# Each expert finishes its own slots: residual rows gathered, normed rows scattered to the output, no combining stage

## The chip, the cores and the metric

One Trainium2 chip, one of its cores. The metric is the device time of one launch in microseconds (us), the median of the runs. The core has a matmul engine (PE, TensorE), a vector engine (DVE), an activation engine (ACT), a general engine (POOL) and a queue that mostly issues transfers (SP). Transfers run on 16 DMA engines that all queues share.

## The reference, cut to what matters

One layer (attention, pooling branch, gated merge) over 576 tokens (512 of a prompt, 64 of samples), width 1024, then a mixture of 32 experts of width 512, two experts for each token. All float32. What the change touches is this end of it:

```python
h  = x + m @ w_out                               # merged branches, residual
xt = rms_norm(h, ffn_norm_g)
g_sel = argmax(xt @ w_router_group + b)          # 4 groups; softmax weight g_w
top_v, top_i = top_k(logits of that group, 2)    # two experts of its 8
e_w = softmax(top_v) * g_w
...
hb = silu(xt[tok] @ w_exp_gate[e]) * (xt[tok] @ w_exp_up[e])
yb = (hb @ w_exp_down[e]) * e_w                  # for each token and chosen expert
h  = h + sum of the token's two yb
y  = rms_norm(h, final_norm_g)                   # y_prompt, y_sample
```

The 32 experts have 1152 assignments, 36 on the mean. The weights of one expert are three blocks (gate, up, down) of 2,048 KB, 192 MiB for all.

## The kernel before, in words

Everything is written by hand for each engine, with semaphores; the order on an engine is the order in the code. The part before the experts (projections, attention, gates, output product) isn't touched, except for a few loads.

**Routing.** For five tiles of 128 tokens, `add_residual` writes h into `resid`; `route` forms the logits. Of the same h, ACT (`xs2`) and POOL (`xn2`, L1821) form the normed rows and POOL stores them to a DRAM tensor `xn2_d` (L1825). DVE chooses experts (`first_of`), ranks each token within its expert, and PE turns that into a table by slot (L991, semaphore `tok_done`): 64 slots (`CAP`) for each expert, and for each slot the row of `xn2_d`. `rowx` and `rowy` are these tables. A slot without a token holds an index out of bounds, for which the transfer moves no row. A branch for experts with over 64 tokens (`over > CAP`) exists and isn't taken on this data.

**Experts.** Expert c uses buffer set s = c mod 2 (`M[s]` holds its semaphores). Rows are handled as halves: partition p < 64 is the first half (512 numbers) of slot p, partition 64 + p the second. For each expert the engines do, in this order:

- POOL `gather_x` (L1701): an indirect DMA of the 128 half rows into `xg[s]`. It is issued as soon as PE has turned the rows of expert c - 2 that were in `xg[s]` (`xt_done`).
- PE `turn_x` (L1001, four transposes), ACT copies to `xT` (L1309).
- PE `gate_up` (L1018): both products into one bank. ACT `silu` (L1313), DVE product (L1647), PE `turn_h` (L1026), ACT copy (L1317), PE `down` (L1033).
- DVE copies the result to `yo[s]` (L1651, semaphore `y_ev`), POOL `scatter_y` (L1705) stores it to its slots in a DRAM tensor `y_d`.

On PE, `turn_x` of expert c + 1 stands between `gate_up` and `turn_h` of expert c. The weights of expert c + 2 are loaded by SP: gate and up (L498, L500) when `gate_up` of expert c is done, down (L503) when `down` of expert c is done. At the start, expert 2's gate goes to a place of its own (`wg2`), its up to `wu2`.

**Combining.** After expert 31, POOL gathers for each of the five tiles the token's two rows of `y_d` (`combine`, L1698, ten indirect DMAs), DVE adds them with their weights to `resid` (L1669), ACT forms the sum of squares and its root (L1350, L1352), DVE the normed rows (L1676), SP stores them (L555).

## Time and profile before

| | |
|---|---|
| median of 3 runs | 1116.12 us (1114.67 to 1117.65) |
| the profiled execution | 1115.16 us, its span 1113.5 us |
| busy in the span: PE, DVE, ACT, POOL | 944.4, 338.7, 201.7, 198.3 us |
| granted TensorE clock, mean | 0.951 of full speed |
| first gate and up product starts | 597.0 us |
| last down product ends | 1079.9 us |
| combining stage, to the end of the span | 33.6 us |

The page of the profile gives busy times over the whole span; which limit holds in which stage is read from the windows, the waits and the timeline.

### The profile page before, as it was taken

To read this page: it belongs to the slowest core of one execution; us is meant where nothing else is said; L and a number is where in the kernel's file an instruction comes from. 1 tells how busy PE (TensorE), PEld (TensorE's weight loads), DVE (VectorE), ACT (ScalarE), POOL (GpSimd) and SP (SyncE) were. 2 spreads that over 40 slices of the span, in tenths; PEclk is the share of its full clock that TensorE was granted. 3 is DMA by queue.
4 is the path that set the end of the run, shared out by engine and by line. 5 is a ranking of instruction groups with operands and counts; after the bars stand their busy time and mean duration, and the time that the engine had idled before them with its cause. 6 is when DMAs were issued, how large, how long until landed. Compare 5 with 4: busy or idle time off the path is not lost.

```text
span 1113.5 us, 11556 instructions
## 1 busy us (share of the span) xinstructions
PE 944.4 (85%) x4412; PEld 510.2 (46%) x4412; DVE 338.7 (30%) x743; ACT 201.7 (18%) x445; POOL 198.3 (18%) x296
## 2 busy tenths in 40 slices
PE   7978999999999998999976998788778887887770
PEld 6633444767776566774543433333233333333220
DVE  2269999973331111330143100000000000000006
ACT  3243111213344233000121000000000000000012
POOL 2730650100001200000231121111110111011113
PEclk9989999999999999999996999999999999899995
DMA  9920221610204527913035999999999999999937
GB/s 335 392 78 1 76 85 38 231 39 38 76 1 152 203 100 216 378 64 150 38 126 227 408 419 426 421 424 425 426 423 424 424 425 425 421 425 425 422 136 252
DMA packets 51814, 283.72 MB, mean 255 GB/s; under 512 B 8476, under 2 KB 9344, under 8 KB 32823
## 3 DMA queue, kind: packets, MB, share of 16 engines
q1 hardware_dynamic: 40935, 246.21, 55.0%
q0 software_dynamic: 10784, 36.97, 9.2%
q8 instruction: 25, 0.41, 0.2%
q14 instruction: 14, 0.11, 0.0%
q10 hardware_dynamic: 56, 0.01, 0.0%
HBM read 267.38 MB, written 23.17 MB: 261 GB/s over the span
## 4 chain that ended last, share of the span: by engine, by line
PE 64%; DVE 18%; issue 7%; ACT 4%; DMA 3%; SPq 2%; POOL 1%; ACTq 0%; POOLq 0%; DVEq 0%
PE psum L1018 21%; PE psum L1033 11%; PE psum L780 9%; DVE arena L1421 6%; DVE arena L1419 6%; PE psum L934 5%; PE psum L916 3%; PE psum L604 3%; DMA arena<-in_w_branch_pool 2%; PE psum L1026 1%; PE psum L868 1%; DVE arena L1647 1%; ACT arena L1313 1%; ACT arena L1317 1%; PE psum L834 1%
## 5 line engine op out<-in xcount | busy, mean ns | idle before, releaser
L1018 PE MATMUL psum<-arena 128*64 128x512 f32 x992 | 238.9, 637 | 56.5 <-issue 55.6
L1018 PEld LDWEIGHTS psum<-arena 128*64 128x64 f32 x992 | 86.2, 147 | 207.5 <-issue 207.5
L1033 PE MATMUL psum<-arena 128*64 128x512 f32 x512 | 116.9, 597 | 17.7 <-ACT arena L1317 17.7
L780 PE MATMUL psum<-arena 128*128 128x288 f32 x480 | 126.1, 416 | 0.0
L780 PEld LDWEIGHTS psum<-arena 128*128 128x128 f32 x480 | 89.6, 192 | 31.0 <-issue 8.1
L1647 DVE TENSOR_TENSOR arena<-arena,psum 128x256 f32<-128x256 f32 x32 | 13.5, 421 | 292.1 <-ACT arena L1313 292.1
L1313 ACT ACTIVATE arena<-psum 128x256 f32<-128x256 f32 x32 | 12.3, 384 | 418.1 <-PE psum L1018 407.3
L590 PE MATMUL psum<-arena 128*128 128x512 f32 x192 | 86.2, 604 | 2.1 <-ACT arena L1184 2.1
L1033 PEld LDWEIGHTS psum<-arena 128*64 128x64 f32 x512 | 40.4, 136 | 72.1 <-issue 72.1
L1651 DVE COPY arena<-psum 128x512 f32<-128x512 f32 x32 | 22.1, 691 | 157.1 <-PE psum L1033 157.1
L916 PE MATMUL psum<-arena 128*128 128x288 f32 x256 | 64.3, 415 | 3.7 <-DMA arena<-in_w_branch_pool 3.7
L1419 DVE MAX8 arena<-arena 64x8 f32<-64x1032 f32 (+3 forms) x80 | 66.2, 828 | 2.8
L1845 POOL CAST arena<-arena 128x1 int32 x30 | 5.6, 185 | 329.7 <-DVE arena L1651 329.7
L1421 DVE MATCH_REPLACE8 arena<-arena 64x1032 f32<-64x1032 f32 (+3 forms) x76 | 61.9, 814 | 0.0
L916 PEld LDWEIGHTS psum<-arena 128*128 128x128 f32 x256 | 49.5, 194 | 18.5 <-DMA arena<-in_w_branch_pool 4.6
L590 PEld LDWEIGHTS psum<-arena 128*128 128x128 f32 x192 | 36.3, 193 | 45.1 <-issue 42.8
L934 PE MATMUL psum<-arena 128*128 128x512 f32 x128 | 55.8, 593 | 1.1 <-issue 1.1
L1091 ACT COPY arena<-psum 128x512 f32<-128x512 f32 (+6 forms) x106 | 47.0, 490 | 53.8 <-PE psum L807 31.8
L1701 POOL DMA_INDIRECT arena<-xn_d,arena x32 | 33.4, 1043 | 33.8 <-POOL arena L1839 25.9
L1705 POOL DMA_INDIRECT y_d<-arena x32 | 33.2, 1037 | 29.0 <-POOL arena L1845 27.4
L934 PEld LDWEIGHTS psum<-arena 128*128 128x128 f32 x128 | 23.9, 190 | 29.7 <-issue 29.7
L1821 POOL TENSOR_TENSOR arena<-arena 128x1024 f32<-128x1024 f32 (+1 forms) x5 | 11.7, 2344 | 139.0 <-ACT arena L1301 139.0
(263 smaller groups left out, 930.8 us busy)
## 6 DMA issues: line engine op xcount, KB each, us to landing
arena<-in_w_exp_down SPq DMA_DIRECT2D x32, 2048.0 KB, 22.9
arena<-in_w_exp_gate SPq DMA_DIRECT2D x31, 2048.0 KB, 18.2
arena<-in_w_exp_up SPq DMA_DIRECT2D x30, 2048.0 KB, 22.6
arena<-in_w_in SPq DMA_DIRECT2D x7, 2048.0 KB, 8.6
y_d<-arena SPq DMA_DIRECT2D x1, 8192.0 KB
arena<-in_x_prompt SPq DMA_DIRECT2D x8, 512.0 KB, 7.2
arena<-in_w_out SPq DMA_DIRECT2D x2, 2048.0 KB, 10.4
arena<-in_w_exp_up SPq DMA_DIRECT2D x4, 1024.0 KB, 12.8
```

The costliest lines, as they stand in the source:

```text
L590: last = pe.matmul(bank(b, n, slice(0, r)), lhs, w[:, k, 0:n], start=(k == 0), stop=(k == KD - 1))
L604: last = pe.matmul(out, lhs, wqi[:, k, QIH * half:QIH * half + QIH], start=(k == 0), stop=(k == KD - 1))
L780: last = pe.matmul(bank(2 + n % 2 if n < SAMPLE_G else 2, HN), ring[slot % 2][:, k, m * P:(m + 1) * P], xnT[:, k, HN * hh:HN * hh + HN], s ...
L916: last = pe.matmul(bank(b, HN), w[:, 4 * br + k, m * P:(m + 1) * P], src[:, k, tc], start=(k == 0), stop=(k == 3))
L934: last = pe.matmul(bank(4 + 2 * (i % 2) + half), sgA[k][:, i * P:(i + 1) * P], ring[(R_OUT + half) % 2][:, k, :], start=(k == 0), stop=(k ...
L1018: last = pe.matmul(bank(2 + s, 512, rows).rearrange("p (w n) -> p w n", w=2), x_k, wgu[s][:, :, DE * k + 256 * q:DE * k + 256 * q + 256], ...
L1033: last = pe.matmul(bank(4 + s, 512, slice(64 * half, 64 * half + 64)), hT[s][:, k % 2, CAP * (k // 2):CAP * (k // 2) + CAP], wd[s][:, k, 5 ...
L1091: last = act.copy(out, src(b))
L1419: link(dve.max(m8, src))
L1421: link(dve.match_replace(w, m8, src, LOW))
L1701: pool.indirect_dma_start(xg[s], None, xn2_d, bass.IndirectOffsetOnAxis(ap=sidx[s], axis=0), bounds_check=2 * NT - 1, oob_is_err=False).th ...
L1705: pool.indirect_dma_start(y_halves, bass.IndirectOffsetOnAxis(ap=syid[s], axis=0), yo[s], None, bounds_check=2 * FIRST - 1, oob_is_err=Fal ...
```

## The change

The sum of the two experts and the final norm move into the expert loop. A token's expert with the lower number ("first visit") adds its weighted result to h and stores the sum to `y_d` at the slot that the token has in its second expert; the expert with the higher number ("second visit") gathers that row as its base, adds its own result, norms it and scatters it straight to the output.

- `xn2_d` is gone: h itself is stored (`h_d`). POOL's five products and ACT's five scalings go; norm factor and expert weight of each slot reach the experts as a table (`weights`, `cur[s]`), made by a second pass of small products on PE (`by_slot`, semaphores `qv_ready`, `qv_done`); silu and the product with up take the norm factor as a scale. The gain is applied as `xT` is written, now by DVE (`take_x`).
- `turn_x`: 16 products of 64x64 in place of 4 transposes of 128x128.
- In the loop, new: `gather_b` (base rows into the same `xg[s]`, after `xt_done`; a first visit's base rows are the h rows that `gather_x` brought), the addition on DVE (L1702 of the new kernel; waits for `b_in`), Square on ACT, `pair_sum` on PE (adds the two half rows' sums; it stands in the middle of the next expert's `gate_up`), Sqrt on ACT, reciprocal and product on DVE, two scatters `scatter_out` (prompt rows, sample rows). Gone: `combine` and all behind it.
- `gather_x` of expert c + 2 now waits for `y_ev` of expert c, since `xg[s]` is read by the addition. `gather_b` of expert c + 1 waits for the landing of `scatter_y` of expert c (`y_st`).
- SP: the rest of expert 1's and expert 2's up weights are loaded without waiting for the row store or the first gathers; expert 2's down (`wd2`) and expert 3's gate (`wg3`) get places of their own and are loaded once `xg_in` of expert 1 has come.

```diff
-            load_expert(1, 0, gate=False, up=False)
...
+            sp.dma_start(by_half(wd2), d_v[2]).then_inc(M[0]["wd_in"], 16)
+            sp.wait_ge(M[1]["wg_in"], 16)
+            sp.dma_start(flat(wg3), g_v[3]).then_inc(M[1]["wg_in"], 16)
...
+                    if prev is not None and k == 4:
+                        pair_sum(*prev)
...
+            def norm(m, s, n, c):
+                act.wait_ge(m["y_ev"], n + 1)
+                act.activation(bank(7), yo[s], ACT.Square, accum_out=sse[:, s:s + 1]).then_inc(S["sq3"], 1)
+                act.wait_ge(S["ps3"], c + 1)
+                act.activation(rte[:, s:s + 1], bank(6, 1, at0=s), ACT.Sqrt, bias=eps, scale=1.0 / D).then_inc(S["rt3"], 1)
...
+            def expert_y(m, s, n, c):
                 dve.wait_ge(m["y_done"], n + 1)
+                dve.wait_ge(m["b_in"], 16 * (n + 1))
...
+                dve.scalar_tensor_tensor(yo[s], bank(4 + s), cur[s][:, 0:1], xg[s], ALU.mult, ALU.add).then_inc(m["y_ev"], 1)
+                dve.wait_ge(S["rt3"], c + 1)
+                dve.reciprocal(rse[:, s:s + 1], rte[:, s:s + 1]).then_inc(S["rs3"], 1)
...
+                dve.scalar_tensor_tensor(fo[s], yo[s], rse[:, s:s + 1], fg2, ALU.mult, ALU.mult).then_inc(m["fin"], 1)
...
+                if more == 2:
+                    pool.wait_ge(M[s]["xt_done"], n + 1)
+                    pool.sem_inc(S["passed"], 1)
+                    pool.tensor_copy(sidx[s], rowx[:, bass.ds(c + 2, 1)]).then_inc(S["sidx_set"], 1)
+                    pool.wait_ge(S["sidx_set"], 2 * c + 2)
+                    pool.wait_ge(M[s]["y_ev"], n + 1)
                     pool.sem_inc(S["passed"], 1)
                     gather_x(s, M[s]["xg_in"])
...
+                scatter_y(s, M[s]["y_st"], FIRST)
+                if more == 2:
+                    pool.tensor_copy(cur[s], weights[:, bass.ds(c + 2, 1), :].squeeze(1)).then_inc(M[s]["c_set"], 1)
+                if more:
+                    if s or not first:
+                        pool.wait_ge(M[t]["o_st"], 32 * (n + s))
+                        pool.sem_inc(S["passed"], 1)
+                    pool.tensor_copy(so[t], rows4[:, bass.ds(c + 1, 1), :].squeeze(1)).then_inc(S["sidx_set"], 1)
+                    pool.wait_ge(S["sidx_set"], 2 * c + 3 if more == 2 else 2 * c + 2)
+                    pool.wait_ge(M[t]["xt_done"], n + s + 1)
+                    pool.wait_ge(M[s]["y_st"], 16 * (n + 1))
                     pool.sem_inc(S["passed"], 1)
+                    gather_b(t, M[t]["b_in"], FIRST)
+                pool.wait_ge(M[s]["fin"], n + 1)
+                pool.sem_inc(S["passed"], 1)
+                scatter_out(s, M[s]["o_st"])
```

POOL in the loop over pairs of experts, first half of the body, before (L1701 is `gather_x` of expert c + 2, L1705 `scatter_y` of expert c; xt_done0 and y_ev0 are those of expert c):

```order
L1839 ISA [waits xt_done0]
L1839 COPY arena<-arena 128x1
L1840 ISA
L1701 DMA arena<-xn_d,arena 128x512 [waits sidx_set]
L1845 ISA [waits y_ev0]
L1845 COPY arena<-arena 128x1
L1846 REGISTER_ALU
L1705 DMA y_d<-arena 36864x512 [waits sidx_set]
```

The same place now (L1756 `gather_x` of expert c + 2, L1764 `scatter_y` of expert c, L1760 `gather_b` of expert c + 1, L1769 the two `scatter_out` of expert c):

```order
L1906 ISA [waits xt_done0]
L1756 DMA arena<-h_d,arena 128x512 [waits sidx_set,y_ev0]
L1764 DMA y_d<-arena 36864x512
L1916 COPY arena<-arena 128x2
L1921 ISA [waits o_st1]
L1921 COPY arena<-arena 128x4
L1924 REGISTER_ALU [waits xt_done1,sidx_set]
L1760 DMA arena<-y_d,arena 128x512 [waits y_st0]
L1769 DMA out<-arena 1024x512 [waits fin0]
L1769 DMA out<-arena 128x512
```

The gather moved from before the wait for `y_ev` to behind it, and a gather stands behind a wait for the scatter's landing; an expert has five indirect DMAs in place of two.

DVE in the loop now, one expert (L1694 product with up, L1670 `take_x` of the next expert, L1702 the addition, L1709 the normed row); before, these were L1647 and L1651 alone:

```order
L1694 SCALAR_TENSOR_TENSOR arena<-psum,arena 128x256 [waits silu0]
L1670 TENSOR_TENSOR arena<-psum,arena 128x512 [waits xt_done1]
L1698 REGISTER_ALU [waits y_done0]
L1700 REGISTER_ALU [waits b_in0]
L1702 SCALAR_TENSOR_TENSOR arena<-psum,arena 128x512 [waits y_st0]
L1704 RECIPROCAL arena<-arena 128x1 [waits rt3]
L1709 SCALAR_TENSOR_TENSOR arena<-arena 128x512 [waits o_st0]
```

The result of an expert now waits for its base rows (`b_in`), which before no engine did.

## Rows read from the trace of the kernel before

**Rows 1.** Windows: 20 experts in mid-loop, then the combining stage; columns in the first row.

```profile
core 0: us, PE busy (x) PEld busy (x) DVE busy (x) ACT busy (x) POOL busy (x), PEclk, DMA share, GB/s
718.84:1034.44 315.60, 251.36 (x1080) 98.14 (x1080) 22.25 (x40) 26.86 (x60) 49.28 (x80) 0.95 1.01 424
...
1080.00:1113.50 33.50, 0.00 (x0) 0.00 (x0) 20.05 (x21) 7.22 (x15) 12.33 (x12) 0.55 0.66 216
```

**Rows 2.** Waits of PE from 700 to 1080 us: total, times, longest.

```profile
PE psum L1018 <- issue: 53.0, 22, 3.3
```

**Rows 3.** Timeline of one expert, mid-loop: start, us, engine, line, idle before.

```profile
1036.61 1.04 POOL L1705 DMA_INDIRECT y_d<-arena  x1 [0.91 <-POOL arena L1845]
1037.51 7.09 PE L1018 MATMUL psum<-arena 128*64 128x512 f32 x32 [3.07 <-issue]
...
1038.71 1.04 POOL L1701 DMA_INDIRECT arena<-xn_d,arena  x1 [0.86 <-POOL arena L1839]
1044.53 0.75 PE L1001 MATMUL psum<-arena 128*128 128x128 f32 x4
...
1045.62 0.48 PE L1026 MATMUL psum<-arena 128*128 128x128 f32 x2 [0.34 <-DVE arena L1647]
...
1046.65 3.65 PE L1033 MATMUL psum<-arena 128*64 128x512 f32 x16 [0.55 <-ACT arena L1317]
...
1050.34 0.69 DVE L1651 COPY arena<-psum 128x512 f32<-128x512 f32 x1 [4.87 <-PE psum L1033]
```

**Rows 4.** Timeline of SP: weight loads issued in the first 100 us of experts.

```profile
595.97 0.33 SPq L518 DMA_DIRECT2D arena<-in_w_exp_up  x1
596.34 0.43 SPq L519 DMA_DIRECT2D arena<-in_w_exp_up  x1
606.71 0.33 SPq L523 DMA_DIRECT2D arena<-in_w_exp_gate  x1
```

**Rows 5.** Line L1701 (`gather_x`), all 32: time from issue to landing.

```profile
DMA to landing us min/median/max: 2.9/8.9/9.8
```

**Rows 6.** Line L1705 (`scatter_y`), all 32: time from issue to landing.

```profile
DMA to landing us min/median/max: 2.4/8.1/8.8
```

**Rows 7.** Line L1701, window 597 to 598: the gather issued at 597.5.

```profile
DMA to landing us min/median/max: 6.2/6.2/6.2
```

**Rows 8.** Line L1705, window 1069 to 1070: the scatter of expert 30.

```profile
DMA to landing us min/median/max: 4.5/4.5/4.5
```

**Rows 9.** Timeline from the slot table to the end of the first gate and up product.

```profile
588.07 2.35 PE L991 MATMUL psum<-arena 128*64 128x32 f32 x40 [2.15 <-DVE arena L1607]
...
591.16 0.32 DVE L1612 TENSOR_TENSOR arena<-arena 128x160 f32<-128x160 f32 x1
...
594.47 0.17 DVE L1638 TENSOR_SCALAR arena<-arena 128x5 f32<-128x5 f32 x1
594.68 0.16 DVE L1640 TENSOR_TENSOR arena<-arena 128x5 f32<-128x5 f32 x1
...
595.16 1.10 PE L1001 MATMUL psum<-arena 128*128 128x128 f32 x4 [4.74 <-DMA arena<-xn_d,arena]
...
597.03 9.65 PE L1018 MATMUL psum<-arena 128*64 128x512 f32 x32 [0.77 <-ACT arena L1309]
```

**Rows 10.** Timeline of the end: last down product, combining stage.

```profile
1076.26 3.65 PE L1033 MATMUL psum<-arena 128*64 128x512 f32 x16 [0.55 <-ACT arena L1317]
1076.67 1.28 ACT L1343 ACT_TABLE_LOAD   x1 [0.56 <-issue]
...
1079.95 0.69 DVE L1651 COPY arena<-psum 128x512 f32<-128x512 f32 x1 [4.86 <-PE psum L1033]
...
1084.64 0.97 POOL L1698 DMA_INDIRECT arena<-y_d,arena  x1 [0.30 <-issue]
...
1097.77 1.03 ACT L1350 ACTIVATE psum<-arena 128x1024 f32<-128x1024 f32 x1 [19.60 <-DVE arena L1669]
...
1098.95 0.29 ACT L1352 ACTIVATE arena<-arena 128x1 f32<-128x1 f32 x1
```

More of the change, by code:

```diff
@@ L304, in program @@
         o = SG + 128
[L305 to L306 removed]
+        trash = at(W1 - D, D)
         xn2T = [at(o + 3 * D + s * D, KD, P) for s in range(2)]
@@ L999, in turn_x, with pair_sum, gate_up @@
                 pe.sem_inc(S["passed"], 1)
-                for t in range(KD // 2):
-                    last = pe.transpose(bank(0, P, at0=t * P), xg[s][:, t:KD // 2 * (P - 1) + t + 1:KD // 2], ident)
+                for k in range(KD):
+                    for half in range(2):
+                        rows = slice(CAP * half, CAP * half + CAP)
+                        last = pe.matmul(bank(0, CAP, rows, k * CAP), xg[s][rows, k:KD * (CAP - 1) + k + 1:KD], ident[rows, rows], start=True, stop=True)
                 last.then_inc(m["xt_done"], 1)
-            def gate_up(m, s, n, third=False, halves=False):
+            def pair_sum(s, c):
+                pe.wait_ge(S["sq3"], c + 1)
+                pe.matmul(bank(6, 1, at0=s), pairs, sse[:, s:s + 1], start=True, stop=True).then_inc(S["ps3"], 1)
+            def gate_up(m, s, n, gate=None, up=None, halves=False, prev=None):
                 pe.wait_ge(m["xt_ev"], n + 1)
@@ L1638, in _ @@
[L1638 to L1644 removed]
+            dve.tensor_tensor(top2, const("valid"), top1, ALU.subtract)
+            dve.tensor_tensor(w1, w1, const("valid"), ALU.mult)
@@ L1651, in expert @@
-                dve.tensor_copy(yo[s], bank(4 + s)).then_inc(m["y_ev"], 1)
-            for s in range(2):
-                expert(M[s], s, 0)
-            with dve.Fori(1, NE // 2) as i:
-                for s in range(2):
-                    expert(M[s], s, i, 16 * i)
+                dve.wait_ge(m["b_in"], 16 * (n + 1))
+                if not (isinstance(n, int) and n == 0):
+                    dve.wait_ge(m["y_st"], 16 * n)
+                dve.sem_inc(S["passed"], 1)
+                dve.scalar_tensor_tensor(yo[s], bank(4 + s), cur[s][:, 0:1], xg[s], ALU.mult, ALU.add).then_inc(m["y_ev"], 1)
@@ new lines, in _, with expert @@
+            pool.wait_ge(M[0]["xt_done"], 1)
+            gather_b(0, M[0]["b_in"], FIRST)
+            def expert(s, n, more=2):
+                c = 2 * n + s
+                t = 1 - s
+                first = isinstance(n, int) and n == 0
+                if more == 2:
[4 more added lines that the diff above has]
+                    pool.wait_ge(M[s]["y_ev"], n + 1)
@@ L1853, in _ @@
-                scatter_y(s, M[s]["y_st"])
-            pool.wait_ge(S["dest_ready"], 1)
+                expert(s, 0)
+            with pool.Fori(1, NE // 2 - 1) as i:
+                for s in range(2):
+                    expert(s, i)
+            expert(0, NE // 2 - 1, 1)
+            expert(1, NE // 2 - 1, 0)
+            for s in range(2):
+                pool.wait_ge(M[s]["y_st"], 16 * (NE // 2))
+                pool.wait_ge(M[s]["o_st"], 32 * (NE // 2))
             pool.wait_ge(S["flag_ready"], 1)
```

499 lines of the change are left out of this document (264 added, 235 removed).

## The prediction

> **What bounds the kernel now.** The windows come first. In mid-loop 20 experts take 315.6 us, 15.78 each, with a DMA share of 1.01 at 424 GB/s [rows 1]. An expert's three weight blocks are 6.29 MB, at 424 GB/s 14.84 us; so 0.94 us of each 15.78 goes to one gather and one scatter. PE isn't the bound: in each expert it waits about 3 us ahead of `gate_up` (53.0 us in 22 times, [rows 2]), put down to "issue", because the weights' landing isn't seen as a releaser. Its own work is 7.09 + 0.75 + 0.48 + 3.65 with gaps, from 1037.51 to 1050.30 in the timeline, 12.8 us [rows 3]. POOL's transfers are off the path: a scatter takes 8.1 us at the median to land and a gather 8.9 [rows 5, 6], but nobody waits for the scatter, and the gather issued at 1038.71 lands some 9 us later for a `turn_x` that is due with the next expert. Behind the last down product (ends 1079.9) stands the combining stage, 33.6 us to the end of the span, nothing else beside it [rows 1, 10].
>
> **The end: removed and added.** The stage is gone. In its place, after expert 31's down product: addition 0.1 + 0.7 (as L1651), Square of half the width of L1350's 1.03, so 0.6 with 0.2 for its sum; then a table load of 1.28 (the Sqrt isn't in silu's table; `pair_sum` lies beside it), Sqrt 0.3, reciprocal 0.15, product 0.7; POOL's pick-up 0.9 (the 0.91 ahead of a DMA in [rows 3]); two scatters, the second 0.97 + 0.30 after the first [rows 10]; landing 2.4, the value without weight traffic [rows 6]; about 1 of gaps. That is 0.85 to the sum and some 9.5 from there. Alone this would save 33.6 - 10.4 = 23 us.
>
> **The start.** The slot table is out of PE at 590.4 and read by 590.9. Then DVE has about 19 small operations, half of them chained at 0.2 apart, and six products of 160 columns at 0.32 or, unchained, a little less: 2.8 + 1.6, `qv_ready` at 595.3 [rows 9]. PE's second pass is 40 products like L991's (2.35 us for 32 columns; now 96, I take 2.6): 598.1. It stands ahead of `turn_x`. Then 16 small products 1.1 (L991's pace, 59 ns each, would give 0.94) and `take_x` 0.7 + 0.2: the first `gate_up` at 600.1 in place of 597.03, +3.1. It takes the same 9.65 [rows 9]: done at 609.8. From `turn_x` to the end of `down` is 5.8 us [rows 3]; 16 products for 4 transposes add 0.4: 6.2. Addition 0.9. Expert 0's sum is ready ("y") at 616.9. POOL's five products and ACT's scalings were beside the routing on DVE and PE: nothing.
>
> **The loop: two circles that the change closes.** Before, no transfer of expert c waited for a result of expert c - 1. Now POOL does, from y of expert c: pick-up 0.9; issue of `gather_x`(c+2) 1.04; 0.3; issue of `scatter_y`(c) at 2.25; **its landing**; pick-up 0.9; `gather_b`(c+1), **its landing**; then 0.85 for the addition: y of c + 1. With unloaded landings (2.4, 2.9) that is 9.3 us. With loaded ones: the scatter now follows a gather by 1.35 us, and of two such transfers the second lands 2.9 us after the first (issued 2.10 apart in [rows 3], landing 8.1 and 8.9), so its own landing takes 9.5; the gather takes 8.1: 2.25 + 9.5 + 0.9 + 8.1 + 0.85 = 21.6 us. The second circle: y of c, 0.9, `gather_x`(c+2) lands (8.1 loaded), `turn_x` to `down` of c + 1 6.3, 0.85: 16.2 loaded, 11.0 unloaded. PE's own work grows to 13.2.
>
> The DMA engines need 14.84 + the small ones. Five in place of two, three of them half filled: between 0.94 + 0.17 (by bytes) and 5 x 0.47 (by number), I take 1.5: 16.3 us for an expert.
>
> Neither 21.6 nor 9.3 can last. At 21.6 the engines would be idle 5.3 us of each, and the landings short; below 16.3 the queue fills up and the landings grow. I lay out one round from y of c. The `pair_sum` wait holds `gate_up`(c+1) in its middle until y + 1.3, its second half is 3.55, so gate and up of c + 3 are issued at y + 4.9 and flow from about 6. If the queue has just run empty before, at 5.5 to 6, gather and scatter land with its end, near 6.8. How a landing shrinks as the backlog ends is seen twice: 6.2 for the gather issued 1.2 us behind two half blocks, 4.5 for the scatter of expert 30 behind the last down block [rows 4, 7, 8]. But `gather_b` is issued at 6.8 + 0.9, into 9.9 us of gate and up, and is fully loaded: 15.8. Then 0.85: y of c + 1 at 16.7. An idle half microsecond on top of 16.3 is what this needs, so the round settles at **16.8 us**. The bounds: 14.8 (landing at 4.8, as unloaded, the gather still loaded) and 21.6.
>
> ACT's table loads (1.28 each, [rows 10], now two an expert) lie in its idle time: silu's is done before `gate_up` ends, Sqrt's while PE is busy; if not covered, up to 1.3 us an expert. `scatter_out` is issued while `gather_b` is under way, so POOL isn't late; it only lengthens the queue. Behind POOL's wait for the landing stand `gather_b` and both `scatter_out`; DVE waits for the former, and through `pair_sum` so does PE.
>
> **Preloads.** Two blocks are 9.9 us of DMA work, moved into the stretch 596 to 607, which holds only the two half blocks now [rows 4]. Where the DMA bounds the loop they are a gain of that size. Where the circle does, they leave the queue empty during experts 1 to 4, which then run at PE's 13.0: 4 x 3.8 = 15 us less.
>
> **Sum.** 616.9 + 31 x 16.8 - 15 + 9.5 = 1132 us of span; the execution's own time is 1.7 above its span (1115.16 to 1113.5), and lies 1.0 below the median: about **1134 us**, 1.6% slower. In terms of before: -23 at the end, +4 to expert 0's sum, +38 from there to expert 31's.
>
> **A rule against the trace.** The landings of the small transfers have medians of 8.1 and 8.9 us under weight traffic and minima of 2.4 and 2.9 [rows 5, 6]. The Trainium skill (DMA: Bandwidth & Descriptors, section Anatomy of one DMA) gives a transfer of this kind as about 2.0 us plus bytes over 436 GB/s, an estimate of 2.3 for the 147 KB of 36 rows. By it the first circle would be 2.25 + 2.3 + 0.9 + 2.3 + 0.85 = 8.6 and never bind; the medians here contradict that, the minima agree. The same page (Issuing engines are not separate DMA queues) has transfers of all queues interleave on the same 16 engines, as the medians suggest.
>
> **Rivals.**
> *The circle hides behind the DMA, faster.* If landings shrink enough (half-empty transfers, idle moments), the loop stays DMA-bound. The last down product ends at 1079.9 now [rows 10]; -9.9 by the preloads, +0.5 x 27 for added traffic, +3 from the later start: it ends about 1087, + 0.85 + 9.5 = 1097, time **1099**. For it: the DMA share of 1.01 says only the queue counts now. Against: it needs the circle under 16.3 with a queue that never empties, in which both landings take over 8. It decides where the two landings together are below 12.3 us. Chance 0.25.
> *The circle is fully loaded, slower.* If the queue's weight packets hold each small transfer its full 8 to 9 us even where the engines are partly idle, 19 to 21.6 a round: 616.9 + 31 x 20 - 20 + 9.5, time **1228**. Chance 0.09.
> *No change.* A circle of 16.2 gives 1115. Chance 0.06.
> My forecast has 0.60.
>
> **Range.** Rounds of 16.3 to 18.0 give 1118 to 1171; with the hidden circle's 1092 to 1105 below, the range is 1092 to 1178; the rest (0.2) is mostly the fully loaded case. The likeliest case's own range is 1120 to 1170. This kernel's measurement tells 0.3%, 3.3 us, from no change. Faster 0.27, same 0.06, slower 0.67.
>
> **What the new profile would show.** Right: in mid-loop a DMA share of 0.95 to 0.98 and rounds near 16.8; DVE's addition waiting for the landing of `gather_b`; PE waiting at `pair_sum`'s line, not ahead of `gate_up`; `scatter_y` landing in some 5 us, `gather_b` in 8; first `gate_up` at 600; 10 us from the last down product to the end. Wrong: a share of 1.00 with PE waiting ahead of `gate_up` (then the circle hides), or `scatter_y` still at 8 us and more beside idle engines (then 20 us rounds).

## The result and the profile after

The changed kernel takes 1187.39 us (median of 4 runs, 1185.81 to 1188.49), the kernel before beside it 1115.72 (1114.67 to 1117.65): ratio 1.0642, 95% interval 1.0628 to 1.0656. It is slower by 71.7 us where 18 were forecast. Its profiled execution has a span of 1186.7 us. One of the four executions of experiment 1 below took 2507 us; the time given there, 1155.8 us, is the median of the other three.

The same stretch of mid-loop as in [rows 1], by windows (PE, PEld, DVE, ACT and POOL busy, granted clock, DMA share, GB/s):

```profile
718.84:1034.44 315.60, 266.21 (x1460) 114.94 (x1460) 48.53 (x87) 75.09 (x120) 99.19 (x138) 0.88 0.93 367
```

The DMA engines, full before at 1.01 and 424 GB/s, now have gaps (0.93, 367), and TensorE's granted clock has fallen from 0.95 to 0.88. So something waits; the question is in which circle.

The addition that makes an expert's sum y (L1702), all 32, by the view of one line: its duration and first and last start, then what ended VectorE's idle time before it:

```profile
L1702 DVE SCALAR_TENSOR_TENSOR arena<-psum,arena x32: 750/751/752, 616.4 to 1171.5; 128x512 f32<-128x512 f32 x32
its engine sat idle before it (us, times) until:
  DMA arena<-y_d,arena: 116.9, 17
  PE psum L1061: 87.5, 15
```

These rows give the two facts on which the rest stands. From the first to the last y are 555.1 us, 31 rounds of **17.91 us**. And 17 times y waited last for `gather_b` (the first circle), 15 times for `down` on TensorE. By the timeline (expert 0's y ends no round) the 17 rounds that end with `gather_b` take 18.5 us at the mean (16.2 to 20.6), the 14 others 17.2 (13.3 to 19.0). Two successive rounds of mid-loop, timeline (start, us, engine, line, idle before):

```profile
871.86 0.75 DVE L1702 SCALAR_TENSOR_TENSOR arena<-psum,arena 128x512 f32<-128x512 f32 x1 [7.17 <-DMA arena<-y_d,arena]
...
873.42 0.38 PE L1027 MATMUL psum<-arena 128*128 128x1 f32 x2 [1.38 <-ACT psum L1349]
873.48 1.06 POOL L1756 DMA_INDIRECT arena<-h_d,arena  x1 [6.57 <-DVE arena L1702]
...
874.85 1.02 POOL L1764 DMA_INDIRECT y_d<-arena  x1 [0.31 <-issue]
...
880.14 2.18 PE L1022 MATMUL psum<-arena 64*64 64x64 f32 x32 [2.75 <-DMA arena<-h_d,arena]
881.03 1.06 POOL L1760 DMA_INDIRECT arena<-y_d,arena  x1 [4.74 <-DMA y_d<-arena]
...
883.70 6.61 PE L1061 MATMUL psum<-arena 128*64 128x512 f32 x16 [0.75 <-ACT arena L1345]
...
890.49 0.75 DVE L1702 SCALAR_TENSOR_TENSOR arena<-psum,arena 128x512 f32<-128x512 f32 x1 [6.66 <-PE psum L1061]
...
898.82 2.14 PE L1022 MATMUL psum<-arena 64*64 64x64 f32 x32 [1.17 <-DMA arena<-h_d,arena]
899.89 1.05 POOL L1760 DMA_INDIRECT arena<-y_d,arena  x1 [5.08 <-issue]
...
901.94 3.65 PE L1061 MATMUL psum<-arena 128*64 128x512 f32 x16 [0.55 <-ACT arena L1345]
...
908.46 0.75 DVE L1702 SCALAR_TENSOR_TENSOR arena<-psum,arena 128x512 f32<-128x512 f32 x1 [6.53 <-DMA arena<-y_d,arena]
```

The first round (18.63 us) runs over the second circle: `gather_x` issued 0.9 behind y, `turn_x` held up 2.75 by it, then `down` in 6.61 us, and y right behind. The second round (17.97) runs over the first circle: `gather_b` issued at 899.89, y 8.57 later, while `down` had taken 3.65 and was long done. The windows of four TensorE pieces (`turn_x` and `down` of the first round, part of `gate_up` and `down` of the second) show where the 3 us between the two `down` come from:

```profile
880.10:882.30 2.20, 2.16 (x33) 2.08 (x33) 0.00 (x0) 0.00 (x0) 1.06 (x1) 0.50 0.94 402
883.70:890.13 6.43, 6.43 (x16) 2.03 (x18) 0.14 (x1) 0.00 (x0) 1.18 (x2) 0.53 0.93 385
895.00:897.60 2.60, 2.60 (x14) 0.62 (x10) 0.48 (x1) 0.74 (x1) 0.00 (x0) 1.00 0.95 394
901.94:905.40 3.46, 3.46 (x17) 1.41 (x19) 0.00 (x0) 0.00 (x0) 1.49 (x3) 1.00 1.04 440
```

Behind the 2.75 us of waiting the granted clock is 0.50 to 0.53 (1.2 GHz); behind the 1.17 us it is 1.00 (2.4 GHz). `turn_x` takes 2.1 us at either.

TensorE's own waits over 24 experts (700 to 1150 us) are nearly all for `gather_x`, ahead of `turn_x`; those at `pair_sum` (L1027), for the y of the expert before, are few:

```profile
PE psum L1022 <- DMA arena<-h_d,arena: 45.1, 24, 3.4
PE psum L1027 <- ACT psum L1349: 6.8, 6, 3.1
```

The landings are shorter than those of [rows 5, 6]. By the view of line L1756 from 700 to 1060 us, `gather_x`:

```profile
DMA to landing us min/median/max: 4.0/6.5/7.4
```

And by that of L1764, `scatter_y`:

```profile
DMA to landing us min/median/max: 2.8/5.3/7.4
```

The end, by the timeline:

```profile
1175.00 0.75 DVE L1709 SCALAR_TENSOR_TENSOR arena<-arena 128x512 f32<-128x512 f32 x1 [0.17 <-DVE arena L1704]
1176.62 0.98 POOL L1769 DMA_INDIRECT out<-arena  x1 [2.48 <-DVE arena L1709]
1177.91 0.98 POOL L1769 DMA_INDIRECT out<-arena  x1 [0.30 <-issue]
```

And by the view of line L146, where each engine's program ends, POOL's row (duration in ns, start):

```profile
L146 POOLq DRAIN  x1: 4709/4709/4709, 1181.7 to 1181.7; - x1
```

From the last y (done at 1172.3) to the end of the span are 14.4 us, 4.7 of them POOL's closing drain.

### The profile page after: what moved, and what is told of

It is laid out like the page before. It is cut to its first block, busy times and chain, and to the rows that moved or that the text cites. A ratio compares the mean times of both kernels' runs of the same rounds, so it can differ in the third digit from the quotient of the medians.

```text
span 1186.7 us, 14414 instructions
## 1 busy us (share of the span) xinstructions
PE 1031.5 (87%) x5444; PEld 569.7 (48%) x5444; DVE 373.9 (32%) x830; ACT 284.0 (24%) x550; POOL 279.9 (24%) x407
## 4 chain that ended last, share of the span: by engine, by line
PE 40%; DMA 30%; DVE 17%; issue 6%; ACT 2%; SPq 2%; POOL 1%; POOLq 1%; DVEq 0%; ACTq 0%
DMA arena<-y_d,arena 12%; DMA y_d<-arena 9%; PE psum L793 8%; PE psum L1061 6%; DVE arena L1441 6%; DVE arena L1439 6%; DMA arena<-h_d,arena 5%; PE psum L947 5%; PE psum L929 3%; PE psum L1022 3%; PE psum L617 2%; DMA arena<-in_w_branch_pool 2%; DVE arena L1702 2%; PE psum L1045 2%; DMA arena<-in_w_in 1%
## 5 line engine op out<-in xcount | busy, mean ns | idle before, releaser
L1045 PE MATMUL psum<-arena 128*64 128x512 f32 x960 | 219.7, 599 | 0.9 <-DVE arena L1670 0.9
L1061 PE MATMUL psum<-arena 128*64 128x512 f32 x512 | 162.5, 792 | 26.8 <-ACT arena L1345 25.0
L1022 PE MATMUL psum<-arena 64*64 64x64 f32 x1024 | 68.8, 290 | 51.5 <-DMA arena<-h_d,arena 51.5
L793 PEld LDWEIGHTS psum<-arena 128*128 128x128 f32 x480 | 89.4, 192 | 30.9 <-issue 8.3
L1022 PEld LDWEIGHTS psum<-arena 64*64 64x64 f32 x1024 | 64.8, 212 | 77.1 <-issue 77.1
L1702 DVE SCALAR_TENSOR_TENSOR arena<-psum,arena 128x512 f32<-128x512 f32 x32 | 24.0, 751 | 204.4 <-DMA arena<-y_d,arena 116.9
L1756 POOL DMA_INDIRECT arena<-h_d,arena x32 | 34.0, 1062 | 217.8 <-DVE arena L1702 186.8
L1349 ACT ACTIVATE psum<-arena 128x512 f32<-128x512 f32 x32 | 19.2, 601 | 225.4 <-DVE arena L1702 225.4
L1769 POOL DMA_INDIRECT out<-arena x64 | 63.8, 997 | 21.7 <-issue 19.2
L1760 POOL DMA_INDIRECT arena<-y_d,arena x32 | 33.9, 1058 | 148.4 <-DMA y_d<-arena 137.8
L929 PEld LDWEIGHTS psum<-arena 128*128 128x128 f32 x256 | 49.5, 194 | 19.5 <-DMA arena<-in_w_branch_pool 5.7
L603 PEld LDWEIGHTS psum<-arena 128*128 128x128 f32 x192 | 35.7, 190 | 44.0 <-issue 41.7
L1670 DVE TENSOR_TENSOR arena<-psum,arena 128x512 f32<-128x512 f32 x32 | 22.1, 692 | 100.6 <-PE psum L1022 95.6
```

The lines of the kernel that those rows point to most:

```text
L603: last = pe.matmul(bank(b, n, slice(0, r)), lhs, w[:, k, 0:n], start=(k == 0), stop=(k == KD - 1))
L793: last = pe.matmul(bank(2 + n % 2 if n < SAMPLE_G else 2, HN), ring[slot % 2][:, k, m * P:(m + 1) * P], xnT[:, k, HN * hh:HN * hh + HN], s ...
L929: last = pe.matmul(bank(b, HN), w[:, 4 * br + k, m * P:(m + 1) * P], src[:, k, tc], start=(k == 0), stop=(k == 3))
L1022: last = pe.matmul(bank(0, CAP, rows, k * CAP), xg[s][rows, k:KD * (CAP - 1) + k + 1:KD], ident[rows, rows], start=True, stop=True)
L1045: last = pe.matmul(bank(2 + s, 512, rows).rearrange("p (w n) -> p w n", w=2), x_k, wgu[s][:, :, DE * k + 256 * q:DE * k + 256 * q + 256], ...
L1061: last = pe.matmul(bank(4 + s, 512, slice(64 * half, 64 * half + 64)), hT[s][:, k % 2, CAP * (k // 2):CAP * (k // 2) + CAP], w[:, k, 512 * ...
```

## The experiments

Theory A: the first circle (y, `scatter_y`, its landing, `gather_b`, its landing, y) sets the round. Theory B: the second (y, `gather_x`, its landing, `turn_x`, `down`, y). Theory C: TensorE's clock or the traffic of the small transfers. Ratios are to the kernel before, with 95% intervals; a round is the time from first to last y over 31, from the row of its line; "last wait" is how often y waited last for `gather_b` and for `down`, from the same view.

**1. Four gather buffers.** `gather_x` no longer needs y to free its buffer (POOL's loop is written out for it).

```
...
-                    pool.wait_ge(M[s]["y_ev"], n + 1)
-                    gather_x(s, M[s]["xg_in"])
+                    gather_x(s, M[s]["xg_in"], 1 - par)
...
+                pool.wait_ge(M[s]["y_ev"], n + 1)
                 scatter_y(s, M[s]["y_st"], FIRST)
```

> Changed kernel with four gather buffers for the residual rows instead of two, so gather_x of the expert after next is issued before the wait for y (POOL's expert loop is written out, the work is the same). Theory A (the circle y, scatter_y, its landing, gather_b, y sets the round of 17.9): scatter_y now stands directly behind the wait for y, 1.3 us earlier, and circle 2 is gone: rounds 16.6, 1187 - 31 x 1.3 = 1147 us. Theory B (circle 2: y, gather_x, turn_x, down, y sets the round, since turn_x waits 51 us in all for gather_x): that wait goes, rounds fall to the 15.8 of the kernel before, 1187 - 31 x 2.1 = 1122. Theory C (TensorE at the lower clock, or the traffic of five small transfers, sets the round): 1187 within 5.

1155.8 us, 1.0375 (1.0351 to 1.0399); round 16.93. Last wait `gather_b` 28 times, `down` 4: the first circle alone, as A has it. The time lies 9 us above what A gave and 34 above B. `scatter_y` is issued 1.4 us earlier behind y, but takes 1.0 longer to land (line of `scatter_y`, 700 to 1060 us):

```profile
DMA to landing us min/median/max: 5.2/6.3/7.1
```

So issuing it earlier is worth less than the 1.3 us that the expectation took off.

**2. `scatter_y` ahead of `gather_x`** (the two lines change places behind the wait for y).

> Changed kernel with one swap on POOL's queue: scatter_y is issued before gather_x and not behind it. Theory A (circle over scatter_y's landing): scatter_y 1.3 us earlier, 1187 - 31 x 1.3 = 1147 us. Theory B (circle over gather_x and turn_x): gather_x is 1.2 us later, so 1187 + 31 x 1.2 = 1224. Theory C (clock or traffic): 1187 within 5. Both circles near 17 us: between 1165 and 1190, and clearly above the kernel with four gather buffers.

1210.3 us, 1.0858 (1.0839 to 1.0876); round 18.59. The addition's last waits in this kernel, all 32:

```profile
  PE psum L1061: 170.8, 30
  DMA arena<-y_d,arena: 10.7, 2
```

This is slower than A alone (1147) or both circles near 17 us (1165 to 1190) allowed, and 14 us less than B alone gave (1224). The second circle, with `gather_x` 1.3 us later, took nearly every round: A alone is wrong, and the prediction's second circle is too short. The first hardly got shorter, for the landing of `scatter_y` grew from a median of 5.3 us (same view):

```profile
DMA to landing us min/median/max: 6.1/6.2/8.1
```

**3. No landing in the first circle.** `scatter_y` writes another tensor, and `gather_b` doesn't wait for it; left out is what a token's first expert passes on to its second.

```
...
+        z_d = nc.dram_tensor("z_d", (SLOTS, D), F32, kind="Internal").ap()
...
-                pool.indirect_dma_start(y_halves, ...
+                pool.indirect_dma_start(z_halves, ...
...
-                    pool.wait_ge(M[s]["y_st"], 16 * (n + 1))
                     gather_b(t, M[t]["b_in"], FIRST)
```

> Changed kernel in which scatter_y writes another tensor of DRAM, so that gather_b need not wait until it has landed; left out: the share that a token's first expert passes on to its second (gather_b reads rows that nobody wrote in this run). All transfers stay as many and as large. Theory A: the landing of 5 us leaves the circle, and circle 2, forecast at 16.2, is next: 1187 - 31 x 1.7 = 1134 us, gather_b's wait at y goes to nearly nothing. Theory B (circle 2 sets the round already) and C (clock or traffic): 1187 within 5.

1169.5 us, 1.0469 (1.0420 to 1.0519); round 17.26, and TensorE was the last wait every time:

```profile
  PE psum L1063: 179.9, 32
```

The time lies between A (1134) and B or C (1187): the landing is on the path, and behind it stands a second circle of 17.3 and not of the 16.2 forecast.

**4. Both cut.** Four buffers, and no landing in the first circle (with what experiment 3 leaves out).

> Both edits together: four gather buffers, and scatter_y to another tensor whose landing gather_b doesn't wait for (left out: the share that a first expert passes on). Neither circle is left; every small transfer still runs. Theories A and B: rounds fall to what the weights' transfer and TensorE ask, 15.8 as in the kernel before, plus the small transfers' share of 0.5: 617 + 31 x 16.3 + 14.4 = 1137, or 1121 if the small transfers cost the weights nothing. Theory C: 1187 within 5, since neither the traffic nor the clock has changed.

1112.8 us, 0.9979 (0.9962 to 0.9995); round 15.54. The windows of mid-loop:

```profile
718.84:1034.44 315.60, 274.47 (x1660) 123.58 (x1656) 56.38 (x99) 85.35 (x136) 111.17 (x157) 0.98 1.01 419
```

All small transfers run, the engines are full again, and the clock is 0.98. Together: first circle alone 16.9 (or 17.2 with `gather_x` still issued ahead of `scatter_y`, experiment 5), second alone 17.3, both 17.9, neither 15.5. The traffic itself costs little, so that half of theory C falls; what costs is the waiting. Each cut alone gives 18 to 32 us of the 75. Even the 1121 us expected for free traffic was too high, and the first rounds show why: they run ahead on the preloads. The first nine take 14.1 us each, with the DMA engines not full and TensorE at the full clock, waiting only some 0.55 us ahead of `down`. Seven of them:

```profile
623.13:721.64 98.51, 94.64 (x655) 50.40 (x653) 19.90 (x35) 30.78 (x49) 39.97 (x57) 1.00 0.90 363
```

So 14.1 us is what TensorE's own chain takes in this kernel.

**5 and 6. The second circle opened on TensorE.** `turn_x` of expert c + 1 behind `down` of c; then also `scatter_y` first.

```
...
-                    if not (last_pair and s == 1):
-                        turn_x(M[1 - s], 1 - s, i + s)
                     turn_h(m, s, i)
                     down(m, s, i, wd2 if e == 2 else None)
+                    if not (last_pair and s == 1):
+                        turn_x(M[1 - s], 1 - s, i + s)
```

> Changed kernel with one move on TensorE: turn_x of expert c + 1 stands behind the down product of expert c, not ahead of turn_h; POOL's order and all transfers stay. The wait for gather_x then no longer lies between y of c - 1 and y of c. Theory now held (two circles of nearly one length: over scatter_y's landing 16.9, as the four buffers left it, and over gather_x, turn_x at the lower clock and down at the lower clock 17.3, as the kernel without the landing left it; the rounds of 17.9 are what the two make together): only the first circle is left, 617 + 31 x 17.0 + 14.4 = 1158, as with four buffers, and down back near 3.65 us. Rival (the extra buffers helped only by issuing gather_x before scatter_y, which shortened the first circle by 1.3): here gather_x is still issued ahead of scatter_y, so 1187 within 5, or more by the 1.7 us that turn_x and take_x add between two gate_up.

> The same move of turn_x, and scatter_y issued ahead of gather_x. Alone, the second edit made the kernel slower (1210 us) as it lengthened the circle over gather_x. Theory now held: with that circle open the 1.3 us come off the first circle, rounds 15.7 to 16.5 (the landings grow a little as the engines are busier), 617 + 31 x 16.1 + 14.4 = 1130, between 1118 and 1143. Rival (scatter_y first makes landings longer by as much, since what counts is when the queue of weights runs empty): 1155 to 1160, as with turn_x moved alone.

1165.2 us (1.0425, 1.0395 to 1.0455), round 17.16; and 1159.1 (1.0385, 1.0358 to 1.0411), round 16.97. The first is 7 us above the 1158 expected for two circles and far from the rival's 1187: `turn_x` behind `down` opens the second circle. In it `down` is back at the full clock (mid-loop, min/median/max ns):

```profile
L1061 PE MATMUL psum<-arena x288: 592/592/643, 728.5 to 1028.0; 128*64 128x512 f32 x144
```

The second gave only 6 of the 28 expected (the two intervals overlap) and came out where its rival said, 1155 to 1160. The rival's reason is in the trace: issued first, `scatter_y` takes 6.2 us at the median to land (same view), where it took 5.0 behind `gather_x`. Another limit lay just below as well; the last of the next four kernels shows which.

```profile
DMA to landing us min/median/max: 5.5/6.2/6.8
```

**7 and 8. The size of the weights' pieces.** 4 KB pieces in all three blocks, with two buffers and with four; then 8 KB pieces in gate and up, with four buffers, and with experiment 6's order. Each block that is changed comes in two transfers in place of one. The 8 KB form:

```
...
+            def put(dst, src, sem):
+                n = dst.shape[1] // 2
+                for b in range(2):
+                    sp.dma_start(dst[:, n * b:n * b + n], src[:, n * b:n * b + n]).then_inc(sem, 16)
...
-                    sp.dma_start(flat(wg[s]), ...).then_inc(m["wg_in"], 16)
+                    put(flat(wg[s]), ..., m["wg_in"])
```

> Changed kernel in which each expert's weight block comes in two transfers of 4 KB pieces instead of one of 16 KB (gate, up) or 8 KB (down) pieces; bytes, buffers and waits stay. Theory P (a small transfer's packets take turns with weight packets, so the size of those sets its landing under load): gather_b lands in 5 to 6 us instead of 8, gather_x and scatter_y in 4, both circles shorten by 3 or more, 617 + 31 x 15.8 + 14.4 = 1121, bounds 1105 and 1145. Theory Q (a small transfer waits for the bytes issued before it): landings and time as in the changed kernel, 1187 within 6. Should the engines move small pieces more slowly, the DMA share is near 1.00 at under 400 GB/s and the time above that of theory P.

> Four gather buffers (1157 us alone) and 4 KB pieces together. Theory P: the circle over scatter_y's landing falls under what the weights need, so the kernel is bound by the DMA engines again: 617 + 31 x 15.8 + 14.4 = 1121, or 1106 if the early experts run ahead on the preloads. Theory Q: 1157 within 5.

> Four gather buffers, and gate and up blocks in two transfers of 8 KB pieces (the down block's pieces are 8 KB in every kernel). With 16 KB pieces this was 1157, with 4 KB pieces 1135, where the DMA engines were full at 404 GB/s in place of 424. If the landing goes by the size of the weight's pieces and the rate too, 8 KB lies between in landing and near 424 in rate: 1130 within 6. If 4 KB pieces helped by something else that two transfers for each block bring, 1135 or less; if only pieces under 8 KB help, 1150 or more.

> Two gather buffers; turn_x behind down, scatter_y ahead of gather_x (1159 together), and gate and up in 8 KB pieces. If the first circle alone is left and its two landings shorten with the pieces by 1 us a round: 1159 - 31 x 1.0 = 1128, between 1118 and 1140. If TensorE's chain (gate and up, turn_h, down, turn_x, take_x, 15.3 with its waits, and pair_sum's) is what is left: 1150 or more, and TensorE waits for take_x at each gate_up with the landing of gather_b there in time.

| kernel | us | ratio (interval) | round |
|---|---|---|---|
| 4 KB | 1165.6 | 1.0443 (1.0404 to 1.0482) | 17.26 |
| four buffers, 4 KB | 1134.6 | 1.0177 (1.0140 to 1.0213) | 16.08 |
| four buffers, 8 KB | 1125.7 | 1.0085 (1.0072 to 1.0099) | 15.95 |
| late, first, 8 KB | 1158.7 | 1.0396 (1.0376 to 1.0416) | 16.95 |

Pieces of 4 KB take 22 us off the changed kernel and 21 off the one with four buffers, 8 KB takes 30 off the latter. So theory Q (nothing changes) is out, and theory P said too much: it had 1121 where 1165.6 and 1134.6 were measured. Since each block also comes in two transfers in these kernels, the size of the pieces isn't told apart from the number of transfers (the 1125.7 fits both expectations that name them); at equal numbers of gate and up transfers 8 KB is 9 us faster than 4 KB (which splits the down block too). The windows of four buffers with 8 KB:

```profile
718.84:1034.44 315.60, 275.06 (x1624) 125.02 (x1622) 54.75 (x96) 84.98 (x136) 112.60 (x157) 0.96 1.01 410
```

The landing that shortened is not `scatter_y`'s (median 6.7 there) but `gather_b`'s: this kernel's y waits 200.7 us in 28 times for it and in mid-loop is done 7.6 us behind its issue at the mean, 9.1 with 16 KB. In the last kernel of the table the time is that of experiment 6, and the addition waits for `gather_b` for 5.5 us in all:

```profile
  DMA arena<-y_d,arena: 5.5, 10
```

y comes when `take_x`, ahead of it in VectorE's order, is done, and that is when TensorE is. In this order TensorE waits 1.3 us for VectorE ahead of `turn_h` and 0.9 for `take_x` ahead of `gate_up`, which makes its chain 16.5 in place of 14.1, and more where its clock falls: the pieces bring nothing where that is the limit. The same waits stand in experiment 5, so its 17.2 isn't a clean measure of the first circle.

**9. Without the two preloads.** Expert 2's down and expert 3's gate are loaded as in the kernel before; then the same with four buffers and 8 KB pieces.

> Changed kernel without its two more preloaded blocks (expert 2's down and expert 3's gate are loaded where the kernel before loads them). If the circles set the round from expert 1 on, a block that is there earlier brings nothing: 1187 within 4, and the first rounds stay at 18 to 20. If experts 1 to 4 do run ahead on the preloads (the prediction's 15 us, of which the trace after shows little), the time rises by 10 to 15, to 1197 to 1202.

> Four gather buffers and 8 KB pieces (1126 us), without the two more preloaded blocks. In the changed kernel undoing them changed nothing (1184 against 1187). If they pay as soon as the circles no longer set the first rounds: up by the 9.9 us of DMA work they move, 1132 to 1137. If the first rounds are set by the circle here too: 1126 within 3.

1184.4 us (1.0624, 1.0604 to 1.0644) against 1187.4: the preloads bring nothing in the changed kernel. 1130.3 (1.0141, 1.0124 to 1.0157) against 1125.7: with the first circle shortened and the second open they are worth 4.6 us, half of what they move and short of the 6 to 11 expected.

**10. TensorE kept busy, and half of `turn_x`.** More matmuls in front of `turn_x`'s wait, 8 and then 2; half of `turn_x`'s columns (left out: half of each expert's input from the third expert on); both.

```
...
+                        if e != 0:
+                            for k in range(8):
+                                pe.matmul(bank(0, 512, slice(0, CAP)), ident[:, 0:CAP], fg2, start=True, stop=True)
                         turn_x(M[1 - s], 1 - s, i + s)
```

> Changed kernel with 8 more matmuls of TensorE, whose result nobody reads, ahead of turn_x's wait for gather_x (1.8 us at the full clock, in a place where it waits 1.9 us on average). Theory K (TensorE's wait for gather_x lowers its clock, and turn_x at 2.1 and down at 5.4 us then lengthen the second circle by some 3 us): turn_x goes to 1.0 and down towards 3.65, the second circle falls to 14.5 to 15, only the one over scatter_y's landing is left: 17.1 to 17.4 a round, 1160 to 1170. Rival (the clock isn't to be had by this, or the second circle is long by its landing): 1187 or up to 1.8 x 31 more, 1187 to 1240, with down still above 750 ns a matmul.

> As the kernel with 8 more matmuls ahead of turn_x's wait, but with 2: in that run one took 0.86 us in place of the 0.23 assumed, so 2 take 1.7, within TensorE's mean wait of 1.9 us for gather_x. Theory K (the wait lowers the clock, and down at 5.4 lengthens the second circle): down near 3.65, second circle 17.3 - 1.7 = 15.6, the first alone is left at 17.0 to 17.4, time 1160 to 1172. Rival (down's length isn't on the path, since gather_b's landing ends last as often): 1187 within 5.

> Changed kernel in which turn_x from the third expert on turns only half of the columns (left out: the other half of each expert's input), so that it takes 1.07 us and not 2.14. If the second circle binds in part of the rounds: 1.07 off it, 16.2 to 16.3 a round there, the first circle's 17.0 to 17.4 is left, and the lower clock stays: 1165 to 1175. If turn_x is beside the path: 1187 within 5.

> Both: half of turn_x (the same half of each expert's input left out) and 2 more matmuls ahead of its wait. Second circle 14.5; the first alone is left: 1157 to 1168, not below the better of the two single edits by more than 5, since that circle has none of these terms. If the time falls under 1150, the first circle too was held up by TensorE, and the model of two separate circles is wrong.

| kernel | us | ratio (interval) | round | last wait `gather_b`, `down` |
|---|---|---|---|---|
| 8 more | 1278.6 | 1.1459 (1.1442 to 1.1477) | 20.72 | 0, 32 |
| 2 more | 1180.2 | 1.0568 (1.0513 to 1.0623) | 17.65 | 20, 12 |
| half `turn_x` | 1176.6 | 1.0548 (1.0530 to 1.0566) | 17.51 | 21, 11 |
| both | 1186.3 | 1.0624 (1.0606 to 1.0642) | 18.14 | 24, 8 |

With 8 more, TensorE became the bound (they take 6.9 us, not 1.8), but its clock is 1.00 and `down` 3.65; `turn_x`, then `down`, by windows of that kernel:

```profile
905.38:907.50 2.12, 2.12 (x34) 2.05 (x33) 0.00 (x0) 0.00 (x0) 0.00 (x0) 1.00 1.06 448
908.50:911.96 3.46, 3.46 (x17) 1.41 (x19) 0.00 (x0) 0.00 (x0) 0.00 (x0) 1.00 0.64 262
```

So the lower clock goes with TensorE's waits, and `turn_x`'s 2.1 us isn't the clock. But the smaller edits gave 7, 11 and 1 us; the last is within the noise, and only half of `turn_x` came near its range (1165 to 1175). The reason is in the table: as TensorE gets faster, `gather_b` becomes the last wait more often (17, 20, 21, 24 times), and the first circle doesn't stay at 16.9 to 17.2. In the last kernel, where it sets 24 of 32, the round is 18.1 (its profiled execution is the slowest of five, 1192.8 us). Two circles with fixed lengths describe this only to about 1 us. That the first one's landings depend on where the weights, which TensorE releases, stand in the queue is likely, but no run here separates it. The last kernel also still has `down` at 796 ns a matmul in mid-loop, so 2 more matmuls didn't secure the clock there; why they did partly in the kernel with 2 alone (685) stays open.

**11. A quarter of the weights in the loop** (up and down are cut like gate, to 1024 elements of each partition; the rest is left out, for experts 6 to 29).

```
...
-                    load_expert(i, s)
+                    sp.dma_start(flat(wg[s])[:, 0:1024], g_v[bass.ds(e, 1), :, 0:1024].squeeze(0)).then_inc(m["wg_in"], 16)
```

> Changed kernel that loads, for experts 6 to 29, only a quarter of each weight block (left out: the rest, so those experts compute with weights of earlier ones); all small transfers, waits and products stay. If the weights' packets make the small landings long: scatter_y lands in 2.4 to 3, gather_b in 3, the first circle is 9.5 to 10.5, the second 12 to 13.5, and TensorE's chain is left: 14.0 to 14.8 a round for 24 of the experts, 1187 - 24 x 3.3 = 1108, between 1095 and 1120. If the landings are long for another reason (POOL's own making of the descriptors, the pieces of the gathers): landings of 5 and 8 us stay, and the time within 1187 to 1170.

1145.2 us, 1.0256 (1.0233 to 1.0279), round 16.49. The landings of `scatter_y` from 718 to 1034 us:

```profile
DMA to landing us min/median/max: 2.1/2.3/2.8
```

The windows of mid-loop:

```profile
718.84:1034.44 315.60, 286.17 (x1618) 128.62 (x1616) 54.76 (x96) 84.67 (x136) 107.70 (x153) 0.92 0.37 117
```

And what the addition waited for last, over all 32:

```profile
  PE psum L1066: 154.0, 30
  DMA arena<-y_d,arena: 15.6, 2
```

The landings did what was expected: it is the weights' traffic that makes them long (2.3 us in place of 5.3), and neither circle is the limit any more. But the time missed its range by 25 us. With a DMA share of 0.37 and short landings a round is still 16.5, where TensorE's chain was to give 14.0 to 14.8, and did give 14.1 in the first rounds of experiment 4. One piece of the timeline shows the difference (`turn_x` started at 858.98):

```profile
860.90 0.98 POOL L1774 DMA_INDIRECT out<-arena  x1 [0.30 <-issue]
861.05 0.51 PE L1058 MATMUL psum<-arena 128*128 128x128 f32 x2
862.51 0.69 DVE L1675 TENSOR_TENSOR arena<-psum,arena 128x512 f32<-128x512 f32 x1 [2.31 <-PE psum L1027]
862.55 0.37 ACT L1350 COPY arena<-psum 128x256 f32<-128x256 f32 x1 [2.98 <-PE psum L1058]
863.07 5.35 PE L1066 MATMUL psum<-arena 128*64 128x512 f32 x16 [1.51 <-ACT arena L1350]
```

The same place in experiment 4:

```profile
865.38 2.14 PE L1024 MATMUL psum<-arena 64*64 64x64 f32 x32
865.55 0.99 POOL L1776 DMA_INDIRECT out<-arena  x1 [0.30 <-issue]
867.56 0.69 DVE L1674 TENSOR_TENSOR arena<-psum,arena 128x512 f32<-128x512 f32 x1 [0.96 <-PE psum L1024]
867.99 0.37 ACT L1349 COPY arena<-psum 128x256 f32<-128x256 f32 x1 [2.02 <-PE psum L1055]
868.50 3.65 PE L1063 MATMUL psum<-arena 128*64 128x512 f32 x16 [0.55 <-ACT arena L1349]
```

`take_x` starts 2.2 us behind `turn_x`'s start there, and 3.5 here; ACT's copy of `turn_h` is late with it, so TensorE waits 1.5 us ahead of `down` and not 0.55, and `down` then takes 5.35 us, at a granted clock of 0.67 and not 1.00. Those 1.0 and 1.7 us are the difference between 14.1 and 16.7, the length of this round; in other rounds `down` stays at 3.65, and they take 15.0. In 20 of the 21 mid-loop rounds that the timeline shows here, `take_x` starts 0.55 to 0.67 us behind the end of POOL's second output scatter, which in experiment 4 is over before `turn_x` is. The changed kernel has such rounds too: `take_x` starts 2.2 to 3.8 us behind `turn_x` there. So part of TensorE's waiting goes with when POOL issues its transfers. What makes the one hold up the other isn't shown.

## Why the prediction was wrong

*Right.* Expert 0's sum: y at 617.2 for 616.9 (the first `gate_up` started at 602.5 and not at 600.1, behind a second pass of 3.5 for 2.6 and a `turn_x` of 2.1 for 1.1; `gate_up` made it up, with 7.09 at the full clock for 9.65, so the close sum is in part luck). POOL's order and pick-ups: `gather_x` 0.87 and `scatter_y` 2.24 behind y, for 0.9 and 2.25. `scatter_y` lands in 5.3 for 4.5, `gather_b` is fully loaded. The mechanism (circles take the round from the DMA engines) and the direction were right, the DMA share nearly (0.93 for 0.95 to 0.98). The rule of the Trainium skill weighed there (DMA: Bandwidth & Descriptors, section Anatomy of one DMA; 2.3 us for such a transfer) agrees with one run, that with a quarter of the weights (2.3); under the full traffic the landings are 2 to 3 times as long.

*The step that failed* is the term of 31 rounds that "settles at **16.8 us**", measured at 17.91, and with it both circles that it was built from.

The second circle was the larger error: "y of c, 0.9, `gather_x`(c+2) lands (8.1 loaded), `turn_x` to `down` of c + 1 6.3, 0.85: 16.2 loaded", with "PE's own work grows to 13.2", was taken as safely below the first. It is 17.3 alone (experiment 3) and sets 14 of the 31 rounds. The landing was over-sized (6.5) and TensorE's part under-sized by more: from `turn_x`'s start to y's end were 11.1 us in the round of 871.86, not 7.2. `turn_x` is 2.14 and not 1.1, its 16 products standing in the trace as 32 pieces, a size that the trace of before had no row for and that went in as "+0.4". And `down` takes 4.9 to 6.6 us where the clock is down, which the prediction nowhere priced, though it did say that TensorE would wait. It expected the wait at `pair_sum`; the waits are ahead of `turn_x`, 45.1 us against 6.8, and that is the sign in the profile that the second circle was in play. TensorE's own chain, taken as 13.2, is 14.1 with none of this (experiment 4) and 16.5 with late hand-overs and the lower clock (experiment 11).

The first circle was under-sized too: the 17 rounds that it sets take 18.5 at the mean and not 16.8. From `scatter_y`'s issue to `gather_b`'s are 6.8 us for 5.45, and from there to y's end 9.3 for 8.95.

Alone, the circles give 16.9 to 17.3 in experiments 1, 3 and 5, and together 17.9. A likely reason is that each varies from round to round (16.2 to 20.6, and 13.3 to 19.0) and the longer one counts each time; this is argued, not shown.

*The account*, in spans, 1186.7 - 1132.2 = 54.5 us:

| term | forecast | measured | difference |
|---|---|---|---|
| y of expert 0 | 616.9 | 617.2 | 0.3 |
| 31 rounds | 16.8 each | 17.91 each | 34.3 |
| early experts at 13.0, by the preloads | -15 | none | 15 |
| last y to the end | 9.5 | 14.4 | 4.9 |

The second line alone would have left the time inside the range (1118 to 1171 for rounds up to 18.0): with 17.91 a round the sum gives some 1168. Without the 15 us of the third it is 1183, above the top of 1178. The third, "which then run at PE's 13.0", took it that empty queues open both circles. The preloads did leave the engines idle (a DMA share of 0.29 and 0.47 in the second and third round), but the first rounds after y of expert 0 are 20.6, 18.4, 15.1, 18.7: in the second `turn_x` still waited 2.6 us for `gather_x` and `down` took 6.3. With both circles cut the early experts do run at TensorE's chain, 14.1 (experiment 4). The fourth is POOL's closing drain, 4.71 us, for which the sum had no term; before, it took 12.4 us and lay under the combining stage:

```profile
L150 POOLq DRAIN  x1: 12407/12407/12407, 1095.1 to 1095.1; - x1
```

*The rivals.* The hidden circle (1099) is what experiment 4 nearly gives, with both circles cut. The fully loaded one (19 to 21.6 a round) didn't come as a whole, though six of the 31 rounds are that long.

*What would repair it.* Four gather buffers and 8 KB pieces take 61.7 of the 71.7 us back. That kernel is at 1125.7, still 0.85% behind the one before: its DMA engines are full again (1.01), at 410 GB/s, and carry five small transfers an expert, and a round of mid-loop costs half a microsecond more than the 15.8 of [rows 1]. Its y still waits for `gather_b` in 28 of 32 rounds, so the first circle isn't ruled out as its limit. No version that computes the whole result beats the kernel before; experiment 4, which leaves a part out, lies 0.2% under it.

## What to carry to other kernels

Removing a serial stage of 33 us by giving its work to the loop is a gain only if no iteration then waits for the one before; here it closed two circles through DMA landings, and each is paid 31 times. When a change makes TensorE wait inside the loop, price its products at the lower clock too, and list every circle with its part of TensorE's chain in it: circles within 1 us of each other gave a round longer here than either alone. Buffers that let a transfer be issued ahead of the result (32 us here) and weight transfers split into smaller ones (21 to 30 us) are cheap to try before the algorithm is given up.

## What the runs showed of the hardware

- Small indirect transfers land in 2.3 us (median of `scatter_y`) with a quarter of the weights' traffic, and in medians of 5.3 to 8.9 with all of it. Splitting the weight transfers at equal bytes, from 16 to 4 KB pieces, takes 22 us off the whole kernel. Pieces of 4 KB kept the engines' share at 1.03 at only 404 GB/s, 8 KB at 1.01 and 410.
- A scatter issued 1.3 to 1.4 us earlier, ahead of the gather, took 1.0 to 1.2 us longer to land: 6.2 or 6.3 at the median for 5.3 (experiments 1 and 2), 6.2 for 5.0 (experiment 6 against 5).
- 16 turning products on 64 rows take 2.14 us at granted clocks of 0.50 and 1.00, where 4 transposes of 128 rows took 0.75 [rows 3]: the time of these products doesn't follow the clock.
- `down` takes 3.65 us at the full clock and 4.9 to 6.6 where the clock is down. What exactly decides it isn't settled. In the rows shown it stayed up behind a wait of 1.17 us ahead of `turn_x` and 0.55 ahead of `down`, and was down behind 2.75 and 0.75; in the round of 732.68 of the changed kernel it was down (0.68, 5.26 us) behind 0.73 and 0.98.
- VectorE and ACT, idle and with nothing else to wait for in the profile, took up TensorE's results 1 us and more late in experiment 11. VectorE started 0.55 to 0.67 us behind the end of one of POOL's indirect scatters in 20 of 21 rounds. The cause is open.
- POOL's closing drain takes 4.7 us behind the last scatters, and 12.4 in the kernel before; here nothing is left beside it, so it is on the path.
